# First stage of a two-block network: token sums by one-column matmuls, a diagonal for the root's row, and high parts before low parts

## The reference, cut to what matters

```
shift, scale, gate = split(silu(c) @ w_mod + b_mod, 3)
mod_c = silu(c_ctx) @ w_mod[:, :3d] + b_mod[:3d]
hx = x   / sqrt(mean(x*x, -1)     + eps) * norm_w * (1 + scale) + shift
hc = ctx / sqrt(mean(ctx*ctx, -1) + eps) * norm_w * (1 + mod_c[d:2d]) + mod_c[:d]
a_h, a_b, a_c, a_z, q, k, v, r_z = split_in(hx @ w_in)
```

## Time and profile before

| | us |
|---|---|
| runs | 3015.53, 3012.26, 3018.45 |
| median | 3015.53 |
| the profiled execution's own time | 3017.88 |
| its span in the trace | 3016.1 |
| mean granted TensorE clock | 0.995 |
| TensorE busy in the span | 2944.0 (98%) |

### The profile page before, as it was taken

One profiled execution on the slowest core, in us unless ns is written; L12 is line 12 of the kernel. 1 busy time (PEld: TensorE's weight loads), 2 busy tenths in 40 slices (PEclk: granted clock), 3 DMA queues, 4 the chain that ended last, 5 costly groups with the idle time before them and its releaser, 6 DMA issues.

```text
span 3016.1 us, 41519 instructions
## 1 busy us (share of the span) xinstructions
PE 2944.0 (98%) x14681; PEld 2473.6 (82%) x14681; DVE 1828.8 (61%) x2315; ACT 1374.8 (46%) x1898; POOL 111.5 (4%) x114
## 2 busy tenths in 40 slices
PE   7999999999999999999999999999999999999999
PEld 4678887788888889988888799997788888878877
DVE  6878878788774345554445667665544544544464
ACT  6732222433343244434444577674544444434353
POOL 0000000010110000001110000000000000000000
PEclk9999999999999999999999999999999999999999
DMA  7855545444554225543334545555455555555554
GB/s 282 298 187 189 182 180 188 147 167 160 190 187 168 91 99 188 185 137 110 111 112 147 168 152 156 158 157 174 157 185 181 187 182 186 182 191 187 188 177 161
DMA packets 144277, 515.12 MB, mean 171 GB/s; under 512 B 16240, under 2 KB 16288, under 8 KB 142256
## 3 DMA queue, kind: packets, MB, share of 16 engines
q1 hardware_dynamic: 141264, 495.01, 48.9%
q0 software_dynamic: 2912, 18.74, 1.6%
HBM read 511.55 MB, written 2.13 MB: 170 GB/s over the span
## 4 chain that ended last, share of the span: by engine, by line
PE 57%; ACT 2%; issue 2%; DVE 2%; DMA 0%; ACTq 0%; DVEq 0%
PE main L1609 48%; PE main L1602 6%; PE aux L1570 1%; ACT w_hi L584 1%; PE aux L1744 0%; PE aux L1735 0%; DVE w_lo L1005 0%; DMA hankel<-bias_by_distance 0%; PE main L1958 0%; ACT L808 0%; PE aux L1795 0%; PE main L1682 0%; DVE h_lo L1127 0%; DMA bias_by_distance<-ext 0%; DVE act_lo L1109 0%
## 5 line engine op out<-in xcount | busy, mean ns | idle before, releaser
L1005 DVE TENSOR_TENSOR w_lo<-raw,w_hi 128x1024 fp32r<-128x1024 f32 x836 | 1038.9, 1246 | 872.7 <-ACT w_hi L584 862.5
L584 ACT ACTIVATE w_hi<-raw 128x1024 fp32r<-128x1024 f32 x836 | 880.3, 1058 | 1297.9 <-PE main L1609 971.2
L1609 PE MATMUL main<-w_hi,h_hi 128*128 128x512 f32 (+1 forms) x1472 | 561.8, 382 | 6.0 <-DVE h_lo L1269 3.1
L1609 PE MATMUL main<-w_hi,h_lo 128*128 128x512 f32 (+1 forms) x1472 | 552.6, 375 | 0.0
L1609 PE MATMUL main<-w_lo,h_hi 128*128 128x512 f32 (+1 forms) x1472 | 552.3, 375 | 0.0
L1609 PE MATMUL main<-w_hi,act_hi 128*128 128x512 f32 (+1 forms) x1408 | 535.7, 380 | 2.9 <-DVE sT L1183 1.5
L1609 PE MATMUL main<-w_hi,act_lo 128*128 128x512 f32 (+1 forms) x1408 | 528.3, 375 | 0.0
L1609 PE MATMUL main<-w_lo,act_hi 128*128 128x512 f32 (+1 forms) x1408 | 527.8, 375 | 0.0
L1602 PE MATMUL main<-act_hi,w_hi 128*128 128x256 f32 (+1 forms) x960 | 322.6, 336 | 3.7 <-DVE act_lo L1109 2.9
L1602 PE MATMUL main<-act_hi,w_lo 128*128 128x256 f32 (+1 forms) x960 | 320.9, 334 | 0.0
L1602 PE MATMUL main<-act_lo,w_hi 128*128 128x256 f32 (+1 forms) x960 | 319.9, 333 | 0.0
(11 more groups left out here) (270 smaller groups left out, 2487.9 us busy)
## 6 DMA issues: line engine op xcount, KB each, us to landing
raw<-in_w_ffn_up SPq DMA_DIRECT2D x176, 512.0 KB, 3.3
gates<-in_w_side SPq DMA_DIRECT2D x128, 512.0 KB, 3.3
raw<-in_w_in_ret SPq DMA_DIRECT2D x128, 512.0 KB, 4.0
raw<-in_w_in_conv SPq DMA_DIRECT2D x120, 512.0 KB, 4.1
raw<-in_w_out SPq DMA_DIRECT2D x96, 512.0 KB, 3.4
raw<-in_w_ffn_down SPq DMA_DIRECT2D x88, 512.0 KB, 3.3
raw<-in_w_mod SPq DMA_DIRECT2D x64, 512.0 KB, 4.5
raw<-in_w_sb SPq DMA_DIRECT2D x64, 384.0 KB, 3.1
```

What stands on the lines that cost most here:

```text
L584: A(w_hi[:, slot, :], raw[:, slot, :], ACT.Copy).then_inc(hi_split, 1)
L1005: V.tensor_tensor(out=w_lo[:, slot, :], in0=raw[:, slot, :], in1=w_hi[:, slot, :].bitcast(F32), op=ALU.subtract).then_inc(lo_split, 1)
L1609: ins = mm(bank[:, c0:c1], x, w_part[:, slot, j * n + c0:j * n + c1], start=(k == 0 and j == 0 and i == 0), stop=(k == per - 1 and j == 1 ...
```

## The change

The sums take the squares as weights (128 features by 128 tokens) and a single column of ones as moving operand, so `aux[2]` holds one sum per token in its columns 0 to 3 (tokens on partitions). Root and reciprocal are taken on 128x4. DVE multiplies the identity by each of the four columns into `dtmp`, and at step 12 PE multiplies that by the matrix of ones, which puts the row of 512 values on all partitions of `aux[3]`; DVE reads it from there for the products with X, of which the first five stand one step later. PE issues the two high-part matmuls of a step behind a wait for the high split alone, and the two low-part ones behind the wait for the low split; `a_bank` likewise has its two low-part matmuls last.

```diff
-X_AT = {12: 0, 13: 1, 14: 2, 15: 3, 16: 4, 18: 5, 25: 6, 27: 7, 29: 8, 31: 9, 43: 10, 45: 11, 47: 12, 56: 13, 58: 14, 60: 15}
+X_AT = {13: 0, 14: 1, 15: 2, 16: 3, 17: 4, 18: 5, 25: 6, 27: 7, 29: 8, 31: 9, 43: 10, 45: 11, 47: 12, 56: 13, 58: 14, 60: 15}
...
-        zflat = zr[:].rearrange("p t n -> p (t n)")
...
-                    A(zflat, aux[2][:, :], ACT.Sqrt, bias=col("eps"), scale=1.0 / D).then_inc(s["norm_root"], 1)
+                    A(rstd_root[:], aux[2][:, 0:4], ACT.Sqrt, bias=col("eps"), scale=1.0 / D).then_inc(s["norm_root"], 1)
...
                 if q == 11:
                     dve.wait_ge(s["norm_root"], 1)
-                    V.reciprocal(out=dtmp[:], in_=zflat).then_inc(s["norm_rstd"], 1)
+                    V.reciprocal(out=rstd[:], in_=rstd_root[:]).then_inc(s["norm_rstd"], 1)
+                    dve.wait_ge(s["norm_rstd"], 1)
+                    for t in range(4):
+                        ins = V.tensor_scalar(out=dtmp[:, t * P:(t + 1) * P], in0=mat("ident"), scalar1=rstd[:, t:t + 1], scalar2=None, op0=ALU.mult)
+                    ins.then_inc(s["root_diag"], 1)
                 if q in X_AT:
                     if X_AT[q] == 0:
-                        dve.wait_ge(s["norm_rstd"], 1)
+                        dve.wait_ge(s["root_row"], 1)
                     tile = X[:, X_AT[q] * 512:(X_AT[q] + 1) * 512]
-                    V.tensor_tensor(out=tile, in0=tile, in1=dtmp[:], op=ALU.mult).then_inc(s["x_scaled"], 1)
+                    V.tensor_tensor(out=tile, in0=tile, in1=aux[3][:, :], op=ALU.mult).then_inc(s["x_scaled"], 1)
...
                 for j in range(2):
-                    ins = mm(aux[2][:, :], mat("ones"), squared[h % 4][:, j * 512:(j + 1) * 512], start=(h == 0 and j == 0), stop=(h == 7 and j == 1))
+                    for t in range(4):
+                        ins = mm(aux[2][:, t:t + 1], squared[h % 4][:, j * 512 + t * P:j * 512 + (t + 1) * P], mat("ones")[:, 0:1],
+                                 start=(h == 0 and j == 0 and t == 0), stop=(h == 7 and j == 1 and t == 3))
...
                 if t == 0:
                     pe.wait_ge(s["h_ready"], j + 1)
-                    pe.wait_ge(s["a_lo_split"], j + 1)
-                for i in range(2):
-                    kt, w0 = 2 * j + i, i * 512 + sec * P
-                    for n, (x, w_part) in enumerate(((act_hi, a_hi), (act_hi, a_lo), (act_lo, a_hi))):
+                    pe.wait_ge(s["a_hi_split"], j + 1)
+                for n, (x, w_part) in enumerate(((act_hi, a_hi), (act_lo, a_hi), (act_hi, a_lo))):
+                    if t == 0 and n == 2:
+                        pe.wait_ge(s["a_lo_split"], j + 1)
+                    for i in range(2):
+                        kt, w0 = 2 * j + i, i * 512 + sec * P
                         ins = mm(main[t][:, :], w_part[:, j % 2, w0:w0 + P], x[:, kt * 512:(kt + 1) * 512],
                                  start=(kt == 0 and n == 0), stop=(kt == KT - 1 and n == 2))
...
+                if q == 12:
+                    pe.wait_ge(s["root_diag"], 1)
+                    mm(aux[3][:, :], mat("ones"), dtmp[:], start=True, stop=True).then_inc(s["root_row"], 1)
                 if q in TURN_AT:
                     turn(TURN_AT[q])
...
-                pe.wait_ge(lo_split, q + 1)
-                for j in range(2):
-                    kt = 2 * k + j
-                    for w_part in (w_hi, w_lo):
+                for w_part in (w_hi, w_lo):
+                    pe.wait_ge(hi_split if w_part is w_hi else lo_split, q + 1)
+                    for j in range(2):
+                        kt = 2 * k + j
                         ins = mm(aux[i % 2][:, :], c_parts[:, 4 * kt:4 * kt + P], w_part[:, q % SLOTS, j * 512:(j + 1) * 512],
                                  start=(kt == 0 and w_part is w_hi), stop=(kt == KT - 1 and w_part is w_lo))
```

More of the change, by code:

```diff
@@ L299, in build @@
         for n in ("side_col half_a half_d side_used side_sum side_T loads_c loads_p act_chain dve_chain pool_chain "
-                  "consts lgx lgd cx cz csplit a_hi_split a_lo_split a_eaten sq_done sq_used x_scaled md_c md_T md_d mg_s mg_d mg_w mg_in mg1_in norm_sum norm_root norm_rstd xs_a xs_d tmp_a tmp_d "
+                  "consts lgx lgd cx cz root_diag root_row csplit a_hi_split a_lo_split a_eaten sq_done sq_used x_scaled md_c md_T md_d mg_s mg_d mg_w mg_in mg1_in norm_sum norm_root norm_rstd xs_a xs_d tmp_a tmp_d "
                   "wide_in xT_ready h_hi_ready h_ready cv_y cv_q cv_done cf_s cf_q cf_r y_scaled "
```

## The result

The changed kernel takes 3025.86 us (median of 11 runs, 3021.25 to 3029.5), the kernel before 3015.4 us over as many. The ratio is 1.0034 with a 95% interval of 1.0025 to 1.0043: slower by some 10 us. A later set of runs gave 1.0027 (1.0018 to 1.0036), some 8 us. The profiled execution took 3026.27 us, with a span of 3024.5.

What follows compares the result with a forecast made beforehand. A closed ring of weight loads, ACT's high and DVE's low parts, held up by PE's backlog and DVE's reciprocal, bounds the first stage. +0.3 - 0.4 - 1.9 - 0.3 = -2.3, rounded to -2.5: 3013.0 us, range 3009 to 3029.

Steps and rivals of the forecast that it cites:

- rival 1: First-stage sums: PE stays at 1.2 GHz under one-column matmuls; +12 us in all, 3027.5 us, chance 0.36.
- The sums: First stage on PE: 128 records at 0.112 us, 15.9 us in all, 1.7 us more than before.
- the forecast's case: Whole kernel: sums' records 0.11 us apart at full clock, 3013.0 us, own range 3010 to 3016, chance 0.38.
- The weight load as floor: PE's sums: each one-column matmul still drags a full weight load, taken as 0.112 us a record.
- rivals 2 and 3: Sums: loads not overlapping, 0.19 us a record, 3023 us, chance 0.07; or cheap loads, 0.07 us, 3010 us, chance 0.13.
- High parts first: PE's matmul order: piece 8 done 0.3 us later, last piece of the stage some 0.3 us sooner.
- Root and reciprocal: ACT's root 0.69 to 0.30 us, -0.4; DVE's 3.35 us reciprocal replaced by 1.4 us of work, -1.9.
- The new waits: PE at step 12 waits for the diagonal, delaying ACT's piece 16; covered by 0.2 us, costs 1.5 at half clock.
- Rival 4: After 45 us loads are the limit and the reciprocal's gain vanishes: 0 to +1 us, 3016 us, chance 0.06.
- a ring of loads: First stage: weight load, ACT's high part and DVE's low part form a closed ring; any delay delays everything after.

Runs made afterwards that it cites:

- the mixed run: Changed kernel with 128 moving columns in parts 0 to 2 of the sums, one in parts 3 to 7: 3015.66 us, ratio 1.0004 to the kernel before.

## Why the prediction was wrong

The forecast was no measurable change (3013.0); the kernel became slower, which stood as rival 1 at 0.36. The range held the time, because it had been made wide enough for that rival.

- **The step that failed** is the one in **The sums**: a record at 0.112 us. The price was right for 2.4 GHz: with 128 columns the records stood 0.112 apart, with one column 0.106. What failed was to take that clock for granted after part 0: one-column records stood 0.213 us apart through all eight parts, the sums took 26.6 us where 15.9 stood, and piece 8 was done 14.8 us later where 0.3 stood. In the kernel before, the level rose within part 0 under 512 columns; with 128 it rose there too, with one it didn't. "PE is never idle in those 20 us" was my argument for the forecast's case; the run with three wide parts shows the level falling under narrow ones with PE never idle. Why the chip grants the lower level there is not shown, only that it does.
- **Rival 1's working held**: 128 x 0.21 = 26.9 (26.6 measured), piece 8 done at 53.3 (53.4), +14.6 (+14.8), 3027.5 (3025.86). What a load takes does double when the clock is halved.
- **The weight load as floor** held, against rivals 2 and 3. The Trainium skill, page "TensorE: Matmul & The Clock Gate", section "LDWEIGHTS (loading the stationary operand)", gives columns / 1.2 ns, 107 ns for 128 columns; the trace of the mixed run agrees, with 0.106 us at 2.4 GHz and one column. At 1.2 GHz a record took 0.213, which that formula doesn't give.
- **High parts first**: nothing measurable, and the forecast had about nothing (+0.3 and -0.3). Both runs on it agree.
- **Root and reciprocal**: the root 0.26 us for the 0.30 taken, the four products 0.87 in all for 1.0, so 4.63 us between two low parts became 2.41, a gain of 2.2 where 1.9 stood. The extra reciprocal shows that such a gain reaches the end, most or all of it.
- **The new waits**: called covered by 0.2 us. In the run with 128 columns, the forecast's own case, PE did drop to the lower level while waiting and ACT waited 3.97 us for it; but moving the diagonal away gained nothing, because the loads were next.
- **The forecast's own case** is nearly the run with 128 columns. It gave -4.9 us (-7.5 to -2.1 by its interval) for the -2.5 of my sum. The interval holds -2.5, so whether a part is missing from the sum isn't settled.
- **Rival 4** fell: a reciprocal of 512 columns at that place costs 3.0 us of time.

## What to carry to other kernels

Before taking columns away from TensorE, look at what keeps its clock up; here an fp32 matmul with a full weight load and one column cost as much as one with 128, and a stretch of them left or put PE at half its clock, everything between them included. Where a ring of loads sets the pace, a cheaper operation counts only if the clock it ran under survives it, and idle PE time ahead of a burst may be worth filling; the one run of that here is a hint, no proof.

## What the runs showed of the hardware that I had not expected

- PE without a gap, in bursts of one-column matmuls with four of 512 columns between them, ran at 1.2 GHz for 34 us (0.213 us a record, 0.43 to 0.5 a matmul of 512 columns), and fell from 2.4 to 1.2 GHz under them in the mixed run. Before, I had linked the lower level to idle time.
- The same 128 weight loads took 0.213 us each at 1.2 GHz and 0.106 to 0.112 at 2.4: the time of a weight load follows the granted clock.
- Halving the records of the sums (fp32r) changed the time by nothing that can be measured, -0.0004 in the ratio against 128 fp32 columns with the diagonal at the same step; with unused matmuls added ahead of them, the kernel was faster by 0.0017 more (two sets of runs, each interval 0.001 or a little more to either side, so the second step is only just clear of noise).
